# Attention values as stationary operand with an early division, and recurrent heads without drains, in a two-layer decoder step

## What is computed

```python
def mem_attend(cq, mk, mv, q_norm):
    ...
    s = jnp.einsum('blhd,bmhd->bhlm', q, mk.astype(F32)) * MEM_HEAD_DIM ** -0.5
    p = jax.nn.softmax(s, axis=-1)
    return jnp.einsum('bhlm,bmhd->blhd', p, mv.astype(F32)).reshape(B, L, MEM_WIDTH)

def swa_prompt(q, k, v, sinks):
    ...
    p = sink_softmax(jnp.where(mask, s, NEG), sinks)
    o = jnp.einsum('bnkgqs,bnskd->bnqkgd', p, vv)
    return o.reshape(B, L, SW_Q_HEADS * SW_HEAD_DIM)

def hgrn_recurrence(q, k, v, logf, s0):
    ...
        att = jnp.einsum('bhtc,bhsc,bhtsc->bhts', qc, kc, decay)
        o = (jnp.einsum('bhts,bhsv->bhtv', att, vc)
             + jnp.einsum('bhtc,bhcv->bhtv', qc * jnp.exp(cum), s))
        s_new = (jnp.exp(last[:, :, 0, :, None]) * s
                 + jnp.einsum('bhsc,bhsv->bhcv', kc * jnp.exp(last - cum), vc))
```

## Time and profile before

| | |
|---|---|
| median of 3 runs | 2895.19 us (2893.66 to 2902.2) |
| profiled execution, its own time | 2896.55 us |
| its span | 2894.7 us |
| TensorE matmuls busy (PE) | 2719.4 us, 94% |
| weight loads busy (PEld) | 2468.8 us, 85% |
| VectorE busy (DVE) | 1554.7 us, 54% |
| ScalarE busy (ACT) | 811.8 us, 28% |
| GpSimd busy (POOL) | 853.9 us, 29% |
| chain that ended last | PE 80%, PEld 8%, ACT 4%, DVE 3% |

### The profile page before, as it was taken

One profiled execution on the slowest core, in us unless ns is written; L12 is line 12 of the kernel. 1 busy time (PEld: TensorE's weight loads), 2 busy tenths in 40 slices (PEclk: granted clock), 3 DMA queues, 4 the chain that ended last, 5 costly groups with the idle time before them and its releaser, 6 DMA issues.

```text
span 2894.7 us, 42932 instructions
## 1 busy us (share of the span) xinstructions
PE 2719.4 (94%) x16064; PEld 2468.8 (85%) x16064; DVE 1554.7 (54%) x2698; ACT 811.8 (28%) x1438; POOL 853.9 (29%) x522
## 2 busy tenths in 40 slices
PE   5789999999799999999998888898899999999998
PEld 5678888988699999999996778777689999999997
DVE  4234444344536666666664243454536666666665
ACT  4331212112522222222216342444452222222220
POOL 5003322332343334333324100000143333443330
PEclk8889999999899999999998899898899999999999
DMA  4121011101121111111110221101011111112111
GB/s 144 51 59 45 23 52 46 41 20 38 39 72 44 43 43 51 51 43 43 43 52 23 66 81 30 23 12 51 25 50 44 43 43 43 43 54 56 49 30 60
DMA packets 186037, 135.50 MB, mean 47 GB/s; under 512 B 19616, under 2 KB 175456, under 8 KB 185888
## 3 DMA queue, kind: packets, MB, share of 16 engines
q1 hardware_dynamic: 181760, 129.69, 16.2%
q10 hardware_dynamic: 4160, 4.19, 0.5%
HBM read 124.61 MB, written 11.27 MB: 47 GB/s over the span
## 4 chain that ended last, share of the span: by engine, by line
PE 80%; PEld 8%; ACT 4%; DVE 3%; issue 2%; POOL 1%; PEldq 1%; DMA 0%; SPq 0%; ACTq 0%; DVEq 0%
PE ps L1690 45%; PE ps L1748 13%; PE ps L1727 8%; PEld ps L1690 4%; PE ps L1909 2%; PEld ps L2043 2%; POOL w_lo L634 1%; PE ps L1894 1%; PE ps L1883 1%; ACT normed L658 1%; PEld ps L1716 1%; ACT prob L757 1%; ACT w_hi L630 1%; PEldq L1707 1%; PE ps L1741 1%
## 5 line engine op out<-in xcount | busy, mean ns | idle before, releaser
L1173 DVE TENSOR_TENSOR x<-x,ps 128x512 f32<-128x512 f32 (+1 forms) x1086 | 705.7, 683 | 444.8 <-PE ps L1748 371.1
L1690 PE MATMUL ps<-hT_hi,w_hi 128*128 128x352 f32 x2976 | 679.9, 331 | 20.0 <-POOL w_lo L634 19.7
L634 POOL TENSOR_TENSOR w_lo<-w_raw,w_hi 128x1024 fp32r<-128x1024 f32 x150 | 366.3, 2461 | 1052.9 <-ACT w_hi L630 879.9
L1690 PE MATMUL ps<-hT_lo,w_hi 128*128 128x352 f32 x2976 | 672.2, 327 | 0.0
L1690 PE MATMUL ps<-hT_hi,w_lo 128*128 128x352 f32 x2976 | 667.5, 327 | 0.0
L1690 PEld LDWEIGHTS ps<-hT_hi,w_lo 128*128 128x128 f32 x2976 | 532.8, 190 | 57.7 <-issue 0.7
L1690 PEld LDWEIGHTS ps<-hT_hi,w_hi 128*128 128x128 f32 x2976 | 515.0, 192 | 23.8 <-issue 13.0
L1690 PEld LDWEIGHTS ps<-hT_lo,w_hi 128*128 128x128 f32 x2976 | 516.0, 191 | 3.5 <-issue 2.0
L1748 PE MATMUL ps<-w_pair_hi,m_hi_lo 128*128 128x512 f32 x1120 | 350.0, 394 | 0.0
L1098 POOL TENSOR_TENSOR w_pair_lo<-w_pair_sum,w_pair_hi 128x512 fp32r<-128x512 f32 x100 | 128.6, 1294 | 435.3 <-ACT w_pair_hi L658 435.3
L1727 PE MATMUL ps<-w_hi,m_hi_lo 128*128 128x512 f32 (+1 forms) x688 | 232.1, 419 | 19.2 <-POOL w_lo L634 8.6
(11 more groups left out here) (252 smaller groups left out, 3075.0 us busy)
## 6 DMA issues: line engine op xcount, KB each, us to landing
w_raw<-in_w_ffn_in_dram SPq DMA_DIRECT2D x176, 256.0 KB, 3.2
w_pair_raw<-in_w_ffn_out_dram SPq DMA_DIRECT2D x88, 256.0 KB, 4.4
w_raw<-in_w_in_hgrn_dram SPq DMA_DIRECT2D x52, 256.0 KB, 4.7
w_raw<-in_w_out_dram SPq DMA_DIRECT2D x32, 256.0 KB, 3.9
w_raw<-in_w_in_swa_dram SPq DMA_DIRECT2D x24, 256.0 KB, 3.9
x<-in_x_prompt_dram SPq DMA_DIRECT2D x8, 512.0 KB, 9.5
w_raw<-in_w_mem_kv_dram SPq DMA_DIRECT2D x16, 256.0 KB, 6.1
cache<-in_cache_mem_k_dram SPq DMA_DIRECT2D x4, 1024.0 KB, 7.0
```

Source lines behind the costliest of these rows:

```text
L634: nc.gpsimd.tensor_tensor(slot(1, s), raw[:, z, :], slot(0, s).bitcast(F32), ALU.subtract).then_inc(w_lo, 1)
L1173: return V_.tensor_tensor(out, a, b, op)
L1690: return mmul(ps[:, b0 + g, 0:TW], slot(a, s)[:, P * k:P * k + P], hT[b][:, k, TW * g:TW * g + TW], start=m < 3, stop=m >= 69)
```

## The change

Attention: VectorE divides the probabilities in place before they are turned (`prompt_norm`); TensorE's turn waits for that; probT is double, and every second step `prompt_feats` multiplies the values of two rounds with the values as stationary side (64 columns), the two heads of the pair in two column groups of the array, which write features instead of rows into the two halves of one bank. The rows in attn_rows, their transposes and VectorE's wait for them are gone. Recurrence: no drain in a head; the count of `w_used` hangs on the first matmul of a following group; the diagonal goes to banks 3 and 4, and the wait for the additions moves to level 0; ScalarE splits the next weight after the key rows; the blocks for the sample states lie in two partition halves, with two more copies by ScalarE.

```diff
@@ ScalarE
                 if r >= 4:
-                    wait(act, vO, r - 4, "o")
+                    wait(act, vN, r - 4, "p")
...
             def prompt_turn(r):
                 wait(act, aPT, r, "pt")
-                if r >= 1:
-                    wait(act, aPV, r - 1, "pv")
-                A(probT[:, :], ps[:, B_PT, :], ACT.Copy, aC, r, "pt")
+                if r >= 2:
+                    wait(act, aPV, r // 2 - 1, "pv")
+                if r in (1, ROUNDS + 1):
+
+                    act.wait_ge(stored, 16 * (2 if r == 1 else NS0 + 2))
+                A(probT[r % 2][:, :], ps[:, B_PT, :], ACT.Copy, aC, r, "pt")
...
                 A(three(tA[:, :]), fm(0), ACT.Sigmoid, hA, h, "sg")
-                if not last:
-                    pump.upto(n0 + 4)
-                else:
-                    pump.upto(n0 + 3)
+                pump.upto(n0 + 3)
...
                 A(KR[0:TS, 8, :], ps[0:TS, 5, P:2 * P], ACT.Copy, hA, h, "kr")
+                nc.scalar.activation(V[TS:2 * TS, 8, :], ps[0:TS, 5, 0:P], ACT.Copy)
+                A(KR[TS:2 * TS, 8, :], ps[0:TS, 5, P:2 * P], ACT.Copy, hA, h, "kd")
+                if not last:
+                    pump.upto(n0 + 4)
@@ VectorE
-            def prompt_rows(r):
-                c, h2 = 10 * (r % 4), r % 2
-                wait(dve, aPV, r, "pv")
-                if r >= 2:
-
-                    wait(dve, aOT, r // 2 - 1, "ot")
+            def prompt_norm(r):
+                c = 10 * (r % 4)
                 wait(dve, vR, r, "rinv")
-                tt(orow[:, :, 64 * h2:64 * h2 + 64], ps[:, B_RO, P * h2:P * h2 + P].rearrange("p (i d) -> p i d", i=2),
-                   st[:, c + 8:c + 10].unsqueeze(2).to_broadcast([P, 2, HD])).then_inc(vO.sem, 1)
+                pr = prob[:, r % 2, :].rearrange("p (i m) -> p i m", i=2)
+                tt(pr, pr, st[:, c + 8:c + 10].unsqueeze(2).to_broadcast([P, 2, 256])).then_inc(vN.sem, 1)
...
-                    if 3 <= s < ROUNDS + 3:
-                        prompt_rows(ROUNDS * p + s - 3)
-                    if 2 <= s < ROUNDS + 2:
-                        prompt_rinv(ROUNDS * p + s - 2, g is not None)
...
                     if second:
                         second(s, 0)
+                    if 1 <= s < ROUNDS + 1:
+                        prompt_rinv(ROUNDS * p + s - 1, g is not None)
+                        prompt_norm(ROUNDS * p + s - 1)
@@ TensorE
             def prompt_turn(r):
-                wait(pe, aE, r, "exp")
+                wait(pe, vN, r, "p")
...
-            def prompt_rows(r, window):
-                half, q, h2 = at_round(r)
-                wait(pe, aC, r, "pt")
-                if r >= 1:
-                    wait(pe, vO, r - 1, "o")
+            def prompt_feats(p, k, window):
+
+                half, q, _ = at_round(2 * k)
+                wait(pe, aC, ROUNDS * p + 2 * k + 1, "pt")
+                if k:
+                    wait(pe, oV, p, f"{k - 1}")
+                elif p > 2:
+                    wait(pe, oV, p - 1, "7")
                 for i in range(2):
...
                     for c in cs:
-                        hc = slice(P * half + 64 * h2, P * half + 64 * h2 + 64)
-                        rhs = vwin[:, t - 1 + c, hc] if window else vmem[:, c, hc]
-                        ins = mmul(ps[:, B_RO, P * h2 + 64 * i:P * h2 + 64 * i + 64],
-                                   probT[:, 256 * c + P * i:256 * c + P * i + P], rhs,
-                                   start=c == cs[0], stop=c == 1)
+                        for h2 in range(2):
+                            hc = slice(P * half + 64 * h2, P * half + 64 * h2 + 64)
+                            v = vwin[:, tile - 1 + c, hc] if window else vmem[:, c, hc]
+                            ins = mmul(ps[64 * h2:64 * h2 + 64, B_RO, P * i:P * i + P], v,
+                                       probT[h2][:, 256 * c + P * i:256 * c + P * i + P], start=c == cs[0], stop=c == 1)
                 ins.then_inc(aPV.sem, 1)
...
-                    if 3 <= s < ROUNDS + 3:
-                        if s == 3 and p > 2:
-                            wait(pe, oV, p - 1, "7")
-                        if s >= 5:
-                            wait(pe, oV, p, f"{(s - 5) // 2}")
-                        prompt_rows(r - 3, window)
+                    if s >= 4 and s % 2 == 0:
+                        prompt_feats(p, (s - 4) // 2, window)
...
-                    if s >= 4 and s % 2 == 0:
-                        prompt_out(r - 3)
@@ TensorE, hgrn_head
-                    mmul(ps[:, 6 + i // 4, P * (i % 4):P * (i % 4) + P], K[:, P * i:P * i + P], Q[:, P * i:P * i + P],
-                         start=True, stop=True)
+                    ins = mmul(ps[:, 3 + i // 4, P * (i % 4):P * (i % 4) + P], K[:, P * i:P * i + P],
+                               Q[:, P * i:P * i + P], start=True, stop=True)
+                    if h and i == 0:
+
+                        ins.then_inc(w_used, 1)
...
-                feat(j, n0 % 2, 0, hT_, (0, 4))
+                feat(j, n0 % 2, 0, hT_, (0, 4), False)
...
                     if l:
                         wait(pe, hP, h, f"k{l - 1}")
+                    elif h:
+
+                        pe.wait_ge(x_added, (OUT0[0] + 1 + h) * OUTG)
...
-                    ins = mmul(ps[:, 6 + z, :], KR[0:TS, 8, :], VM[0:TS, 512 * z:512 * z + 512], start=True, stop=True)
+                    ins = mmul(ps[:, 6 + z, :], KR[TS * z:TS * z + TS, 8, :], VM[TS * z:TS * z + TS, :], start=True, stop=True)
...
-                used(j + 3)
                 for g in range(g, OUTG):
-                    out_group(G0 + g, g // 2, g % 2, [(0, n0 % 2)])
-                used(j + 4)
-
-                pe.wait_ge(x_added, G0 + OUTG)
+
+                    out_group(G0 + g, g // 2, g % 2, [(0, n0 % 2)], release=g == 10)
```

65 lines of the change are left out of this document (35 added, 30 removed).

## The result

The changed kernel takes 2864.58 us (median of 7 runs, 2861.27 to 2873.62), the kernel before 2894.32 us on the same chips; the ratio is 0.9895, with a 95% interval of 0.9874 to 0.9916. That is 30 us less (24 to 37), where 57.5 were forecast: the direction was right, the time lies at the upper end of the range, the gain is half of the forecast.

The account below looks back on a forecast made before the run. TensorE, busy 94% of the span, was taken as the bound, with engine chains in memory periods. Memory pairs -11.6 and -9.5, window pairs -15.1, heads -21.3 sum to -57.5 from 2896.55: 2839 us, range 2815 to 2866.

Parts of the forecast that it names:

- Heads: Recurrent heads: fewer drains, a later weight split, row groups and a moved wait take off 21.3 us.
- the terms on the boundary, the value features and the row groups: Heads: first matmul's 0.83 us wait goes at five boundaries (4.2); value features give 1.1, sample-state row groups 0.87 per head.
- The rival for this part: Heads: shorter drains uncover VectorE's and GpSimd's level chain, so the heads gain only 15 us; no separate chance given.
- Value products: Attention on TensorE: 16 instructions in two column groups take 1.1 us per two rounds, 0.7 less than now.
- Rival (a): Attention value products: column groups don't overlap, 1.9 us per two rounds, as much as now; about 2863 us in all; 12%.
- Filled periods: Attention periods with other TensorE work: window 9.4 to 9.7 us for 10.07, memory 8.8 for 9.99, taken as -1.0 each.
- Early division: Attention on VectorE: reciprocal, in-place division and handing over put about 1.0 us between exponential and turn, free where TensorE has other work.
- the last 21.3 us: End of the third window pair, without filling: a chain from last scores to next stage, forecast 15.7 us, so -5.5.
- Where projections fill the steps there is no add in front, and the 0.7 stays: Two window pairs, three periods each: the products' whole 0.7 us gain is kept, -4.2 us in all.
- The end of the second memory stage: Second memory pair's end, 20.15 us: two turns come 1.1 us earlier and 0.7 of TensorE's work goes, -2.9.
- (c): Whole kernel: a chain binds again or TensorE's clock falls longer; attention gives 10 us, heads 15, so 2872 us; 12%.

## Why the prediction was right or wrong

**Heads: right.** 21.3 us were forecast, 21.5 stand between the traces, 23 (15 to 31) in the run of the heads alone. That the first two agree to 0.2 us is chance: in the traces of the other kernels with the new heads this stretch takes 1377 to 1392 us. The three rows above answer to the terms on the boundary, the value features and the row groups; no drain stands in a head any more. The rival for this part, that a later wait would take the gaps' place, shows in no row; TensorE's waits of the output groups for the additions (L1727, now L1728) grew by 1 us in the whole execution.

**Value products: right.** 1.03 us for 16 instructions, 1.1 forecast; how much of it is going into the tiled form and back (0.15 and 0.1 in the sum) no run shows. Rival (a) is refuted, although the measured 2864.6 is nearly the time it gave (2863): a time that fits a rival does not make its mechanism true. And it is luck that the time lies in the range, whose upper end, 2866, was put just past this rival's time. By the Trainium skill's "TensorE: Matmul & The Clock Gate" (section "The mechanism"), weight loads overlap matmuls only where row groups differ, though the same section also lets a load into the background weight buffer go ahead. Here they share the rows and differ in columns, and 16 loads with 16 matmuls pass in 1.03 us, against 1.67 at the single pace of the earlier trace rows. The trace does not bear out the first half of this, and the measurement decides.

**Filled periods: right where they were worked out.** 9.20 for a memory period (8.8 forecast, 9.99 before), 9.72 for a window period (9.4 to 9.7, 10.07 before), with 0.2 us of waiting for the division. But the gain of 1.0 us was put down for all seven periods of the second memory stage, and only two of them gave 0.8 and 1.0; the seven together became 3.0 us longer, where 7.0 less were forecast.

**Early division: mis-sized, and the step that failed.** The prediction said that 1.0 us stands between exponential and turn, and then followed it only where TensorE sets the pace. Attention without the division is worth 49 us, and the division costs 41 of them. In the sum it has 0.25 us in each of the twelve filled window periods (0.7 less 0.45), a part of the chain in the memory periods and at the last stage's end, and nothing elsewhere. Three places were missed:

- The empty periods of the last window stage are not in the sum at all. The first had 7.32 us and became 10.40, the next 7.92 and became 10.10; with GpSimd's work cut they were 8.67 and 9.63, without the division 7.68 and 8.72. The prediction called the last 21.3 us a chain and forecast 15.7; it became 18.4, at the lower clock throughout.
- "Where projections fill the steps there is no add in front, and the 0.7 stays" was read from the filling alone. The -4.2 us became -0.7. Behind the last scores of the two stages VectorE has the gain of the next queries and an instruction held by GpSimd in front of a division, and the two ends cost 3.7 and 5.9 us more than without the division. The two periods that grew there did so for another reason, the wait for a weight's low part at a lower clock.
- The end of the second memory stage has the keys' norm in VectorE's queue: the last period went from 10.52 to 14.16, where -1.0 was forecast (11.17 without the division).

Of the rivals (c) comes nearest: a chain binds again, attention gives little (8 measured, 10 there) and the clock falls at the end of the last stage; only its heads were taken too small. It had 12%. What the runs show of the cause: the division's price lies in the order of the engines' programs, since two exchanges of order, with the division left in, take back 36 us, of which some 14 were there to be had before the change. What the division still costs in that order is not shown, for no kernel had the exchanges and no division. The keys' norm and the queries' gains could not be moved to where they cost nothing; whether they could be cut up was not tried.

**GpSimd's hold** was in no step. The Trainium skill, "SBUF — State Buffer", section "Who interferes with whom", says that a VectorE instruction with two SBUF inputs contends with a GpSimd instruction that reads SBUF, and calls the ports that they share an exclusive lock. The trace agrees: 0.16 us became 2.27, and the instruction ended with GpSimd's product; maxima, which read PSUM, ran at their usual 0.48 us in the same stretch. The kernel before had such holds too (1.76 us on 128x2 elements at 2058.85). But its VectorE read the products from PSUM, off the turn's path; the division has two SBUF inputs and small ones ahead of it. By the rule alone, with the 2.3 us of GpSimd's product, five places come to 11 us, an estimate; the run with the work cut gave 9, in which TensorE's own wait for the low part has a share.

## What to carry to other kernels

When an operation moves ahead of another engine's work, follow the loop that it closes in the stretches where nothing fills the engine that was the bound, and list all that stands ahead of it in its new queue; the average of the filled stretches tells neither. Look then for an order that opens the loop, and try that order on the old kernel too: here one exchange on ScalarE was worth nearly as much as the change itself, and half of it had nothing to do with the change. A period that grew is not yet the new operation's price: two of them stayed as long without the division. And a long VectorE job with someone waiting at either side of it gave nothing here when it was moved.

## What the runs showed of the hardware

Two column groups of 64 stationary columns, which share all rows, take 16 loads and 16 matmuls of 128 columns in 1.03 us at the full clock. Two row groups of 32 rows bring four instructions of 512 columns from 1.98 to 1.13 us. A VectorE instruction on 128x2 elements with two inputs in SBUF took 2.27 us and not 0.16 when GpSimd's product ran, and ended with it. A reciprocal of 128x1056 elements takes 6.74 us on VectorE, a product of that size 1.26. At the end of a stage with nothing to fill it, the same 78 matmuls with their waits took 18.4 us at a granted clock of 0.50, and 11.5 at 0.98 in the kernel without the division.
